# Middle stage of a hybrid encoder: 32x32 triangular blocks on GpSimd, half solves and unnormalised keys and queries

## Chip, cores, metric

One core of one Trainium2 chip. The metric is device time in microseconds of one execution of the whole kernel. The kernel before was run three times: 3174.05, 3177.18 and 3189.18 us, median 3177.18.

## What is computed

One layer over 2,064 prompt rows (16 meta tokens and 2,048 inputs) and 32 sample rows: an input projection with a short causal convolution, a gated delta rule (8 heads of 64) beside a sliding-window attention (8 query heads, 2 key/value heads), an output projection, a layer norm, and a squared-ReLU feed-forward block with a second layer norm. The part that the change touches is the delta rule:

```python
q = l2_normalize(q) * DN_DK ** -0.5 ; k = l2_normalize(k)
A = where(strict, beta[..., :, None] * kk * decay, 0)        # kk = k k^T, decay from the cumulated gates
T = A + eye(chunk)
W = triangular_solve(T, beta * exp(G) * k) ; U = triangular_solve(T, beta * v)
qk = (q k^T) * decay ; q_dec = q * exp(G) ; k_dec = k * exp(G_last - G)
# per chunk:  u = U - W S ;  o = q_dec S + qk u ;  S = exp(G_last) S + k_dec^T u
o = o * rsqrt(mean(o^2) + eps) * norm_w * silu(z)
```

The kernel works in chunks of 128 tokens (a tile), so T is 128x128 for each of 8 heads, and the state goes from tile to tile.

## The kernel before

Three stages run one after the other. The first (project_stage) makes the projections, normalises the input and writes everything to scratch in device memory. The middle one (mix_stage) goes over 18 tiles of 128 tokens, two per round of a hardware loop, the first four and the last two tiles written out. The last (mlp_stage) is the feed-forward block. In the middle stage each engine has its own order of work, written out by hand in a function `step(t)`, and semaphores tie them together; nothing is planned by a program. In step t three tiles are in flight: the delta rule and attention of tile t, the preparation (norms, decays, products of keys) of tile n = t+1, and output projection and layer norm of tile p = t-1 (pp = t-2 for its transposed rows). PSUM has eight banks: inv0, inv1, fr0, fr1, prod, pair, one1, one2.

**The inverse of T.** Its 16x16 diagonal blocks (64 lanes: 8 heads by 8 blocks) are inverted on GpSimd by forward substitution, L1710 to L1723: two operations over 64x256, then 28 small ones, each of which waits for the one before it. The lanes get their blocks through device memory. SyncE, which issues all DMAs in its own order, waits for at_done, writes `at` out (L848), waits for that to land, and reads the diagonal back (L850); after GpSimd's last step it writes the blocks (L858), waits, and reads whole 128x128 rows into `nn` (L862). TensorE and VectorE then build 32x32 and 64x64 inverses in two levels: transpose (L1038), product (L1052), mask (VectorE L1365), product (L1060), update (VectorE L1372); and the last level with 64x64 products (L1074, L1083) and copies (L1378, L1384). `solve` (L1111) multiplies the 128x128 inverse with the right-hand side of each head.

**Keys and queries** are normalised before use: ScalarE squares them, TensorE sums squares over a head with a 128x128 mask matrix (L972), ScalarE takes Ln and Exp (L1553 to L1561), VectorE multiplies (L1295). `spread_gates` (L980) spreads cumulated gates over 128 partitions from 8 rows. `turn_keys` (L1007) transposes keys and values.

**Order on SyncE in a step:** load z, load res of p, store rows of pp, to_lanes(n), store columns of pp, load_front (gates and q/k/v of t+2), from_lanes(n), load_attention of t+2. **Order on GpSimd:** small inverses of n, then `low` twice (L1733, remainder of the mixed rows after rounding, needed by the output projection), then the shift of the layer norm of p (L1740). **Order on TensorE:** the step starts with the transpose of the gates of n (L960), then the inverse's levels are laid between pieces of the output projection of p (three_products, L122 to L124) so that VectorE's and ScalarE's work is covered.

Of the kernel before, what the change touches and what calls it, by code (L numbers as in the profile page):

```python
# [48 lines left out]
LEVELS = (16, 32)  # L49
SMALL = 16  # L50
LANES = HEADS * P // SMALL
LANE_STRIDE = SMALL * P + SMALL
# [618 lines left out]
def mix_stage(nc, io):  # L671

    with ExitStack() as ctx:
        m = Memory(nc, ctx, "b")

        masks = m.sb("masks", [P, 4 + len(LEVELS), P])
        ident, upper, same_head, future = (masks[:, i, :] for i in range(4))
        level_mask = [masks[:, 4 + i, :] for i in range(len(LEVELS))]
        pick = m.sb("pick", [HEADS, HEADS, P])
# [6 lines left out]
        consts = m.sb("consts", [P, 3])  # L686
        lane_masks = m.sb("lane_masks", [LANES, 2, SMALL * SMALL])

        qkv = m.sb("qkv", [P, 12, P])
# [5 lines left out]
        gate = m.sb("gate", [P, 2 * HEADS])  # L695
        cum = m.sb("cum", [P, 2, HEADS])
        cum_row = m.sb("cum_row", [HEADS, P])
# [4 lines left out]
        hat = m.sb("hat", [P, 2, 8, P])  # L702
        at = m.sb("at", [P, 2, HEADS, P])
        work = m.sb("work", [P, HEADS, P])
        nn = m.sb("nn", [P, 2, HEADS, P])
# [3 lines left out]
        lane_a = m.sb("lane_a", [LANES, SMALL, SMALL])  # L709
        lane_n = m.sb("lane_n", [LANES, SMALL, SMALL])  # L710
        lane_t = m.sb("lane_t", [LANES, HD])
# [8 lines left out]
        decay, squares = probs_t[:, 0, :, :], probs_t[:, 1, :, :]  # L720
# [3 lines left out]
        mm = turned_rows[:, :, :, :].rearrange("p a h c -> p (a h c)").rearrange("p (h c) -> p h c", c=P)  # L724
# [18 lines left out]

        def turned_heads(bank, g):

            return fr[bank][:, :].rearrange("p (j g c) -> p g j c", g=2, c=HD)[:, g, :, :]

        def odd_blocks(x, l):

            return x.rearrange("p h (n two b) -> p (h n) two b", two=2, b=LEVELS[l])[:, :, 1, :]  # L750

        def whole(scratch):

            return scratch.rearrange("(h b) x -> h (b x)", h=HEADS)[:, 0:P * P].rearrange("h (p i) -> p h i", i=P)

        def diagonal(scratch):

            return scratch[:, 0:SMALL * P].rearrange("l (j i) -> l j i", i=P)[:, :, 0:SMALL]

        names = """const_in wo_in0 wo_in1 bias_out bias_in zero_out qkv_in att_in z_in res_in h1_out h1t_out state_in state_out  # L760
        at_out lanes_in nn_out nn_in rel_full rel_copied wo_hi_done wo_lo_done zeroed window_added hidden_in hidden_done
        gate_full ss_full cum_full gb_full kk_full qk_full scored kv_turned m_full r_full x_full r_end x_end
        ks_full y_full snew_full oin_full vwin_turned pt_full ont_full pv_full wo_full ost_full h1t_full
        gates_copied cum_copied hat_done em_done at_done qk_scaled lane_steps lanes_done kd_done s_biased soft_steps
        r_masked n_done r_end_done n_final rn_first rn_done qs_scaled u_done s_scaled state_done o_done o_summed
        on_done mixd_done attn_scaled soft_end resid_done ln_halves ln_stats ln_shift ln_gain beta_done
        squared ss_logged rnorm_done gate_exps decay_done m_done v_copied probs_done sink_exp pt_copied
# [6 lines left out]
        L = len(LEVELS)  # L774
        TURNS = 2 * L + 2
# [11 lines left out]
        def _(sp):  # L787
            for dst, src in ((masks[:, :, :], io["masks"]), (pick[:, :, :], io["pick"]), (key_mask[:, :], io["window"]),
                             (gain[:, :], io["ln1_g"].partition_broadcast(P)),
                             (shift[:, :], io["ln1_b"].partition_broadcast(P)), (norm_w[:, :], io["norm_w"]),  # L790
                             (sinks[:, :], io["sinks"].partition_broadcast(P)),
                             (lane_masks[:, :, :], io["lane_masks"]),
                             (probs[0:N_BUCKETS, 0, 0:HEADS], io["table"]),
                             (probs_t[0:N_BUCKETS, 0, 0:3, :].rearrange("p a b -> p (a b)")[:, 0:REL], io["one_hot"])):
                sp.dma_start(dst, src).then_inc(s["const_in"], 16)

            def load_front(t):
                if t.reaches(1):
                    q = t.plus(-1)
                    sp.wait_ge(s["kv_turned"], by(q, 2))  # L800
                    pass_waits(sp, s["passed"])
                    sp.wait_ge(s["hat_done"], by(q, 2))
                here = t.span(P)
                sp.dma_start(gate_rows[:, :], io["gates"][:, here]).then_inc(s["qkv_in"], 16)
                sp.dma_start(qkv[:, :, :], io["proj"][0:12, :, here].rearrange("u p c -> p u c")).then_inc(s["qkv_in"], 16)
# [40 lines left out]
            def to_lanes(t):  # L846
                sp.wait_ge(s["at_done"], by(t, 2))
                sp.dma_start(whole(io["at_lanes"]), at[:, t.parity, :, :]).then_inc(s["at_out"], 16)  # L848
                sp.wait_ge(s["at_out"], by(t, 16))
                sp.dma_start(lane_a[:, :, :], diagonal(io["at_lanes"])).then_inc(s["lanes_in"], 16)  # L850

            def from_lanes(t):
                sp.wait_ge(s["lanes_done"], by(t, 1))
                if t.reaches(1):
                    sp.wait_ge(s["nn_in"], by(t.plus(-1), 16))
                else:
                    sp.wait_ge(s["zero_out"], 48)
                sp.dma_start(diagonal(io["nn_lanes"]), lane_n[:, :, :]).then_inc(s["nn_out"], 16)  # L858
                sp.wait_ge(s["nn_out"], by(t, 16))
                if t.reaches(2):  # L860
                    sp.wait_ge(s["y_full"], by(t.plus(-2), 1))
                sp.dma_start(nn[:, t.parity, :, :], whole(io["nn_lanes"])).then_inc(s["nn_in"], 16)  # L862
# [21 lines left out]
            def step(t):  # L884
# [5 lines left out]
                if t.reaches(1):  # L890
                    load_res(t.plus(-1))
                if t.reaches(2):
# [5 lines left out]
                if m2:  # L898
                    load_front(m2)
                if n:  # L900
                    from_lanes(n)
# [6 lines left out]
                if m2:  # L908
                    load_attention(m2)

# [5 lines left out]
            sp.wait_ge(s["zeroed"], 4)  # L916
            empty = work[0:LANES, :, :].rearrange("p a b -> p (a b)")
            for c in range(0, LANE_STRIDE, D_MODEL):
                width = min(D_MODEL, LANE_STRIDE - c)
                sp.dma_start(io["nn_lanes"][:, c:c + width], empty[:, 0:width]).then_inc(s["zero_out"], 16)  # L920
# [28 lines left out]
        def _(pe):  # L949
# [4 lines left out]
            def turn_gates(t):  # L954
                pe.wait_ge(s["qkv_in"], by(t, 32))
                pass_waits(pe, s["passed"])
                if t.reaches(1):
                    pe.wait_ge(s["vwin_copied"], by(t.plus(-1), 1))
                pass_waits(pe, s["passed"])
                pe.transpose(one2[:, 0:2 * HEADS], gate_rows[:, :], ident[0:2 * HEADS, 0:2 * HEADS]).then_inc(s["gate_full"], 1)  # L960

            def sum_gates(t):
                pe.wait_ge(s["gates_copied"], by(t, 1))
                pe.matmul(one2[:, 0:HEADS], upper, gate[:, 0:HEADS], start=True, stop=True)
                pe.matmul(one2[0:HEADS, P:2 * P], gate[:, 0:HEADS], upper, start=True, stop=True).then_inc(s["cum_full"], 1)

            def norms(t):
                if t.reaches(1):
                    pe.wait_ge(s["s_biased"], by(t, 2, 1) if t is START else by(t.plus(-1), 2, 1))
                for g in range(2):  # L970
                    pe.wait_ge(s["squared"], by(t, 2, g + 1))
                    pe.matmul(fr[g][:, :], same_head, squares[:, 4 * g:4 * g + 4, :].rearrange("p a b -> p (a b)"),  # L972
                              start=True, stop=True).then_inc(s["ss_full"], 1)

            def spread_gates(t):
                pe.wait_ge(s["cum_copied"], by(t, 3))
                for g in range(2):
                    pe.wait_ge(s["ss_logged"], by(t, 2, g + 1))
                    for h in range(4):
                        last = pe.matmul(fr[g][:, h * P:h * P + P], pick[:, 4 * g + h, :], cum_row[:, :], start=True, stop=True)  # L980
                    last.then_inc(s["gb_full"], 1)

            def key_products(t):
                pe.wait_ge(s["hat_done"], by(t, 2))
                pe.wait_ge(s["em_done"], by(t, 6))
                for j in range(4):
                    for g in range(2):
                        k = hat[64 * g:64 * g + 64, t.parity, 4 + j, :]
# [4 lines left out]
            def query_products(t):  # L993
                pe.wait_ge(s["at_done"], by(t, 2))
                for j in range(4):
                    for g in range(2):
                        half = slice(64 * g, 64 * g + 64)
                        last = pe.matmul(fr[g][:, j * P:j * P + P], hat[half, t.parity, 4 + j, :], hat[half, t.parity, j, :],
                                         start=True, stop=True)
                last.then_inc(s["qk_full"], 1)  # L1000

            def turn_keys(t):
                pe.wait_ge(s["qk_scaled"], by(t, 1))
                for g in range(2):
                    for j in range(4):
                        src = hat[:, t.parity, 4 + j, :] if g == 0 else qkv[:, 8 + j, :]
                        last = pe.transpose(fr[g][:, j * P:j * P + P], src, ident)  # L1007
                    last.then_inc(s["kv_turned"], 1)

            def scores(t, first=False):  # L1010
# [3 lines left out]
                else:  # L1014
                    pe.wait_ge(s["kd_done"], by(t, 2))
                    pe.wait_ge(s["v_copied"], by(t, 2))
# [9 lines left out]
            def turn_values(t):  # L1026
                if t.reaches(1):
                    pe.wait_ge(s["o_done"], by(t.plus(-1), 1))
                else:
                    pe.wait_ge(s["cum_copied"], by(t, 3))  # L1030
# [4 lines left out]
            def turn_inverse(t, g):  # L1035

                for h in range(4):
                    last = pe.transpose(inv[g][:, h * P:h * P + P], nn[:, t.parity, 4 * g + h, :], ident)  # L1038
                last.then_inc(s["m_full"], 1)

            def first_inverse(t):
# [1156 lines left out]
```

## Time and profile before

| what | value |
|---|---|
| median of the runs | 3177.18 us (3174.05 to 3189.18) |
| the profiled execution | 3180.55 us; its span 3178.8 us |
| TensorE busy | 2939.2 us (92%) |
| VectorE, ScalarE, GpSimd busy | 1355.9, 1006.3, 1205.9 us |
| granted TensorE clock, mean | 0.963 of full speed |
| middle stage | about 612 to 1654 us from the span's start |

Times in the rows are counted from the start of the span. PE is TensorE, DVE VectorE, ACT ScalarE, POOL GpSimd, SPq the queue of SyncE. A matmul of 32-bit numbers has two records per matmul; the output projection works on halves rounded to fp32r and has one. Busy time is the union of the records, which overlap at their ends.

### The profile page before, as it was taken

To read this page: it belongs to the slowest core of one execution; us is meant where nothing else is said; L and a number is where in the kernel's file an instruction comes from. 1 tells how busy PE (TensorE), PEld (TensorE's weight loads), DVE (VectorE), ACT (ScalarE), POOL (GpSimd) and SP (SyncE) were. 2 spreads that over 40 slices of the span, in tenths; PEclk is the share of its full clock that TensorE was granted. 3 is DMA by queue.
4 is the path that set the end of the run, shared out by engine and by line. 5 is a ranking of instruction groups with operands and counts; after the bars stand their busy time and mean duration, and the time that the engine had idled before them with its cause. 6 is when DMAs were issued, how large, how long until landed. Compare 5 with 4: busy or idle time off the path is not lost. (4 is left out here: it accounts for less than half of the span.)

```text
span 3178.8 us, 50801 instructions
## 1 busy us (share of the span) xinstructions
PE 2939.2 (92%) x18048; PEld 2774.9 (87%) x18048; DVE 1355.9 (43%) x2341; ACT 1006.3 (32%) x2072; POOL 1205.9 (38%) x1282
## 2 busy tenths in 40 slices
PE   5899999729999999999959999999999999999997
PEld 4899999618787878878848999999999999999996
DVE  7643200135656565656625511651363156116502
ACT  4322211324434443444422222222222222222222
POOL 4210101012222222222205555555555555555554
PEclk9899999859999999999978999999999999999998
DMA  5322212252232222233214434444444434444432
GB/s 192 116 86 71 86 67 83 64 136 62 87 88 81 83 84 79 87 93 87 76 50 141 135 124 126 130 143 127 134 134 128 134 110 141 139 130 130 133 113 88
DMA packets 238591, 341.83 MB, mean 108 GB/s; under 512 B 56578, under 2 KB 176322, under 8 KB 235674
## 3 DMA queue, kind: packets, MB, share of 16 engines
q1 hardware_dynamic: 237450, 339.01, 34.5%
q10 hardware_dynamic: 1056, 1.70, 0.2%
q8 instruction: 52, 0.85, 0.1%
q14 instruction: 33, 0.27, 0.0%
HBM read 264.45 MB, written 76.21 MB: 107 GB/s over the span
## 5 line engine op out<-in xcount | busy, mean ns | idle before, releaser
L1949 POOL TENSOR_TENSOR c_w_lo<-c_raw,c_w_hi 128x512 fp32r<-128x512 f32 x640 | 852.3, 1332 | 639.2 <-ACT c_w_hi L1969 639.0
L1969 ACT ACTIVATE c_w_hi<-c_raw 128x512 fp32r<-128x512 f32 x640 | 404.3, 632 | 1057.6 <-PE c_bank L124 1024.9
L122 PE MATMUL c_bank<-c_h_hi,c_w_hi 128*128 128x416 f32 x1280 | 454.1, 355 | 20.7 <-POOL c_w_lo L1949 19.5
L124 PE MATMUL c_bank<-c_h_hi,c_w_lo 128*128 128x416 f32 x1280 | 452.8, 354 | 0.0
L124 PE MATMUL c_bank<-c_mid_hi,c_w_lo 128*128 128x416 f32 x1280 | 450.8, 352 | 0.0
L122 PE MATMUL c_bank<-c_mid_hi,c_w_hi 128*128 128x416 f32 x1280 | 450.2, 352 | 0.0
L123 PE MATMUL c_bank<-c_h_lo,c_w_hi 128*128 128x416 f32 x1280 | 449.1, 351 | 0.0
L123 PE MATMUL c_bank<-c_mid_lo,c_w_hi 128*128 128x416 f32 x1280 | 447.0, 349 | 0.0
L122 PE MATMUL a_bank<-a_h_hi,a_w_hi 128*128 128x420 f32 (+4 forms) x984 | 341.3, 347 | 5.9 <-PEq L168 4.5
L124 PE MATMUL a_bank<-a_h_hi,a_w_lo 128*128 128x420 f32 (+4 forms) x984 | 340.0, 346 | 0.0
L123 PE MATMUL a_bank<-a_h_lo,a_w_hi 128*128 128x420 f32 (+4 forms) x984 | 339.8, 345 | 0.0
L2074 DVE COPY c_out<-c_bank 128x416 f32 x40 | 23.7, 591 | 627.2 <-PE c_bank L124 627.2
L122 PEld LDWEIGHTS c_bank<-c_h_hi,c_w_hi 128*128 128x128 f32 x1280 | 241.9, 189 | 22.6 <-POOL c_w_lo L1949 21.1
L124 PEld LDWEIGHTS c_bank<-c_h_hi,c_w_lo 128*128 128x128 f32 x1280 | 241.7, 189 | 3.3
L123 PEld LDWEIGHTS c_bank<-c_h_lo,c_w_hi 128*128 128x128 f32 x1280 | 241.6, 189 | 2.8
L124 PEld LDWEIGHTS c_bank<-c_mid_hi,c_w_lo 128*128 128x128 f32 x1280 | 240.2, 188 | 3.2
L123 PEld LDWEIGHTS c_bank<-c_mid_lo,c_w_hi 128*128 128x128 f32 x1280 | 240.0, 188 | 2.7
L122 PEld LDWEIGHTS c_bank<-c_mid_hi,c_w_hi 128*128 128x128 f32 x1280 | 240.5, 188 | 0.1
L2021 DVE TENSOR_SCALAR c_positive<-c_bank 128x416 f32<-128x416 f32 x160 | 94.4, 590 | 244.9 <-PE c_bank L124 244.9
L527 POOL TENSOR_TENSOR a_w_lo<-a_raw,a_w_hi 128x1024 fp32r<-128x1024 f32 x20 | 48.3, 2413 | 394.4 <-ACT a_w_hi L543 394.4
L122 PEld LDWEIGHTS a_bank<-a_h_hi,a_w_hi 128*128 128x128 f32 x984 | 188.7, 192 | 9.2 <-issue 5.6
L123 PEld LDWEIGHTS a_bank<-a_h_lo,a_w_hi 128*128 128x128 f32 x984 | 188.6, 192 | 3.1
(221 smaller groups left out, 4479.6 us busy)
## 6 DMA issues: line engine op xcount, KB each, us to landing
c_raw<-in_w_ff SPq DMA_DIRECT2D x320, 512.0 KB, 3.6
scratch_proj<-a_row SPq DMA_DIRECT2D x22, 1152.0 KB, 5.1
b_qkv<-scratch_proj SPq DMA_DIRECT2D x18, 768.0 KB, 5.5
a_raw<-in_w_in SPq DMA_DIRECT2D x23, 512.0 KB
a_x<-in_x SPq DMA_DIRECT2D x18, 512.0 KB, 3.6
scratch_h_rows<-a_h SPq DMA_DIRECT2D x18, 512.0 KB, 2.7
scratch_at_lanes<-b_at SPq DMA_DIRECT2D x18, 512.0 KB, 3.2
b_nn<-scratch_nn_lanes SPq DMA_DIRECT2D x18, 512.0 KB, 4.0
```

The lines of the kernel that those rows point to most:

```text
L122: pe.matmul(out, w_hi, x_hi, start=first, stop=False)
L123: pe.matmul(out, w_hi, x_lo, start=False, stop=False)
L124: return pe.matmul(out, w_lo, x_hi, start=False, stop=last)
L527: pool.tensor_tensor(w_lo[:, p, :, :], raw[:, p, :, :], w_hi[:, p, :, :].bitcast(F32), ALU.subtract).then_inc(w_lo_done, 1)
L1949: pool.tensor_tensor(w_lo[:, p % 2, ks, :], raw[:, p, ks, :], w_hi[:, p % 2, ks, :].bitcast(F32), ALU.subtract).then_inc(w_lo_done, 1)
L1969: act.activation(w_hi[:, p % 2, ks, :], raw[:, p, ks, :], ACT.Copy).then_inc(w_hi_done, 1)
L2021: dve.tensor_scalar(positive[:, :], src, 0.0, None, ALU.max).then_inc(positive_done, 1)
L2074: dve.tensor_copy(out[:, one(c2 * 2 + c), :], bank2[c][:, 0:BLOCK].unsqueeze(1)).then_inc(out_done, 1)
```

## The change

- GpSimd inverts 32x32 blocks: 32 of them (8 heads by 4), each spread over four partitions (SHARES) with eight of its columns each, so 128 partitions. 62 small operations in place of 2 + 28, and one copy (set_lanes) ahead of them.
- The blocks travel in four DMAs each way and leg: `at` out by 32-row blocks, four reads of the same blocks into the four shares, four writes of columns, four reads into `nn`, which now holds 64 columns for each half.
- TensorE pairs 32x32 blocks to 64x64 ones (pair_rows, pair_update, 16 matmuls of 32x32x32 each), VectorE transposes the even blocks (turn_even) and copies (copy_pair_rows, place_pair). The solve goes by halves: solve_head (rows 0 to 63), carry_over (the block of `at` below), take_over on VectorE, solve_rest. The levels of masks are gone.
- Keys and queries stay unnormalised in the products; their lengths enter through the strengths, the values (scale_values) and the factor of the output's norm (o_weighed, o_factor). TensorE transposes q, k and v (q is new), ScalarE squares the transposed rows, VectorE sums (sum_keys, sum_queries). The mask product (L972) and the multiplication (L1295) are gone. qkv has two buffers.
- spread_gates takes its rows from partitions 0 to 7 and 64 to 71 in turn.
- `low` moves from GpSimd to VectorE.
- The orders of all engines are rewritten. SyncE: load_front of t+2 comes ahead of to_lanes(n), and from_lanes(n) comes last, after load_attention. scores now comes ahead of attend.

The core of the diff:

```diff
-LEVELS = (16, 32)
-SMALL = 16
-LANES = HEADS * P // SMALL
+SMALL, SHARES = 32, 4
+LANES = HEADS * BLOCKS32
+LANE_COLS = SMALL // SHARES
...
             def to_lanes(t):
                 sp.wait_ge(s["at_done"], by(t, 2))
-                sp.dma_start(whole(io["at_lanes"]), at[:, t.parity, :, :]).then_inc(s["at_out"], 16)
-                sp.wait_ge(s["at_out"], by(t, 16))
-                sp.dma_start(lane_a[:, :, :], diagonal(io["at_lanes"])).then_inc(s["lanes_in"], 16)
+                for b in range(BLOCKS32):
+                    here = slice(b * SMALL, b * SMALL + SMALL)
+                    sp.dma_start(io["at_lanes"][b * HEADS:b * HEADS + HEADS, :, :].rearrange("h j i -> j h i"),
+                                 at[here, t.parity, :, here]).then_inc(s["at_out"], 16)
+                sp.wait_ge(s["at_out"], by(t, 16 * BLOCKS32))
+                for q in range(SHARES):
+                    sp.dma_start(lane_a[q * LANES:q * LANES + LANES, :, :], io["at_lanes"]).then_inc(s["lanes_in"], 16)
...
             def from_lanes(t):
                 sp.wait_ge(s["lanes_done"], by(t, 1))
+                columns = io["nn_lanes"].rearrange("(c q) l r -> q l c r", q=SHARES)
+                for q in range(SHARES):
+                    sp.dma_start(columns[q], lane_n[q * LANES:q * LANES + LANES, :, :]).then_inc(s["nn_out"], 16)
+                sp.wait_ge(s["nn_out"], by(t, LANE_LOADS))
...
+                for b in range(BLOCKS32):
+                    half = slice(b % 2 * SMALL, b % 2 * SMALL + SMALL)
+                    sp.dma_start(nn[b * SMALL:b * SMALL + SMALL, t.parity, :, half],
+                                 io["nn_lanes"][:, b * HEADS:b * HEADS + HEADS, :]).then_inc(s["nn_in"], 16)
...
+                for j in range(SMALL - 1):
+                    w, n = SMALL - 1 - j, j // SHARES + 1
+                    shape = [P, n, w]
+                    here = lane_n[:, 0:n, j + 1:SMALL]
...
+            def turn_even(t):
+                dve.wait_ge(s["nn_in"], by(t, LANE_LOADS))
+                dve.transpose(nn_even[:, :, :], nn[:, t.parity, :, 0:SMALL]).then_inc(s["even_turned"], 1)
+            def take_over(t):
+                dve.wait_ge(s["low_full"], by(t, 1))
+                dve.tensor_tensor(rn[64:P, :, :], rn[64:P, :, :], heads4(one2, HD)[64:P, :, :], ALU.add).then_inc(s["low_done"], 1)
```

The new order of a step on SyncE, TensorE and VectorE (`if` lines left out):

```python
# SyncE
load_z(t); load_res(p); load_front(t+2); store_rows(pp); to_lanes(n); store_cols(pp); load_attention(t+2); from_lanes(n)
# TensorE
turn_gates(n); turn_rows k, v (n); sum_gates(n); from_state(t); spread_gates(n); turn_queries(n)
output_product(p, 0, ATTENTION); key_products(n); turn_h1(pp, 0); output_product(p, 0, DELTA); pair_rows(t)
turn_h1(pp, 1); output_product(p, 1, ATTENTION); pair_update(t); query_products(n); solve_head(t)
output_product(p, 1, 0:2); carry_over(t); output_product(p, 1, 2:4); solve_rest(t); turn_probs(t, 0 and 1)
state_update(t); output_update(t); scores(n); attend(t); turn_values(n); turn_o(t); turn_attention(t)
# VectorE
copy_gates(n); low(p); copy_sums(n); low(p); sum_keys(n); residue(t); strengths(n); exponents(n); scale_values(n)
sum_queries(n); decayed_keys(n); turn_even(t); residual(p, 0); copy_pair_rows(t); left_keys(n); maxima(t)
place_pair(t); decayed_queries(n); take_over(t); residual(p, 1); update(t); softmax_sums(t); norm_stats(p)
new_state(t); new_output(t); norm_shift(p); sum_squares(t); biased(n); normalise_o(t); norm_gain(p)
scale_attention(t); gate_o(t)
# GpSimd
set_lanes(n); small_inverses(n); h1_rows(p)
```

## Rows read from the trace of the kernel before

**Rows 1.** Engines by stretch: the middle stage's start and its steady part (busy us, records).
```profile
612.00:706.30 94.30, 19.12 (x89) 12.43 (x87) 24.42 (x49) 19.78 (x40) 10.36 (x30) 0.55 0.55 128
805.00:1560.50 755.50, 717.27 (x5781) 611.61 (x5780) 463.87 (x1017) 331.24 (x875) 199.49 (x485) 0.98 0.29 85
```
**Rows 2.** The same view (PE, PEld, DVE, ACT, POOL, PEclk, DMA, GB/s), two steps.
```profile
1010.96:1063.25 52.29, 49.74 (x397) 41.96 (x396) 31.55 (x70) 22.47 (x59) 13.47 (x33) 0.97 0.28 83
1063.25:1113.83 50.58, 48.03 (x396) 41.35 (x395) 31.53 (x70) 22.36 (x59) 13.44 (x33) 1.00 0.30 86
```
**Rows 3.** One line's instructions: the transpose of the gates, one in each step.
```profile
L960 PE MATMUL b_one<-b_masks,b_gate_rows x18: 230/231/256, 636.9 to 1526.4; 16*128 16x16 f32 x18
```
**Rows 4.** Groups of TensorE in 1010.96:1113.83, two steps: count, busy, mean ns, idle before.
```profile
L1052 PE MATMUL b_inv<-b_turned_rows,b_at 128*128 128x128 f32 x64 | 8.2, 281 | 0.0
L1060 PE MATMUL b_inv<-b_nn,b_work 128*128 128x128 f32 x64 | 8.0, 278 | 0.0
...
L1038 PE MATMUL b_inv<-b_masks,b_nn 128*128 128x128 f32 x48 | 6.4, 276 | 2.7 <-DVE b_probs L1341 2.7
L972 PE MATMUL b_fr<-b_probs_t,b_masks 128*128 128x512 f32 x8 | 5.6, 838 | 1.2 <-ACT b_probs_t L1547 1.2
L980 PE MATMUL b_fr<-b_cum_row,b_pick 8*128 8x128 f32 x32 | 4.1, 276 | 0.0
L1102 PE MATMUL b_one<-b_state,b_hat 64*128 64x64 f32 x64 | 4.0, 275 | 0.0
...
L1111 PE MATMUL b_one<-b_rn,b_nn 128*128 128x64 f32 x32 | 3.8, 272 | 0.0
...
L1074 PE MATMUL b_inv<-b_turned_rows,b_at 64*64 64x64 f32 x32 | 2.3, 220 | 0.7 <-ACT b_turned_rows L1584 0.7
```
**Rows 5.** GpSimd in order of time (start, us), smallest and largest steps of one inversion.
```profile
885.59 0.20 POOL L1720 TENSOR_TENSOR b_lane_t<-b_lane_a,b_lane_n 64x14 f32<-64x14 f32 x1
885.87 0.21 POOL L1723 TENSOR_TENSOR b_lane_n<-b_lane_n,b_lane_t 64x14 f32<-64x14 f32 x1
...
889.90 0.29 POOL L1723 TENSOR_TENSOR b_lane_n<-b_lane_n,b_lane_t 64x56 f32<-64x56 f32 x1
890.27 0.28 POOL L1720 TENSOR_TENSOR b_lane_t<-b_lane_a,b_lane_n 64x56 f32<-64x56 f32 x1
```
**Rows 6.** TensorE in order of time: its first record of tile 0's delta rule.
```profile
706.27 1.94 PE L1038 MATMUL b_inv<-b_masks,b_nn 128*128 128x128 f32 x8 [16.50 <-DMA b_nn<-scratch_nn_lanes]
```
**Rows 7.** VectorE and GpSimd in order of time, first tile's inversion.
```profile
694.44 1.24 DVE L1474 TENSOR_TENSOR b_wo_lo<-b_x,b_wo_hi 128x1024 fp32r<-128x1024 f32 x1 [5.98 <-ACT b_wo_hi L1650]
...
694.67 1.14 POOL L1723 TENSOR_TENSOR b_lane_n<-b_lane_n,b_lane_t 64x44 f32<-64x44 f32 x1
```
**Rows 8.** Groups of VectorE in 833:1600 that read two operands from SBUF.
```profile
L1357 DVE TENSOR_TENSOR b_soft<-b_soft,b_sinks 128x8 f32<-128x8 f32 x15 | 20.0, 1336 | 0.5
...
L1470 DVE TENSOR_TENSOR b_x<-b_x,b_gain 128x1024 f32<-128x1024 f32 x15 | 18.2, 1215 | 0.0
```
**Rows 9.** SyncE's queue in order of time: issues around one inversion.
```profile
1031.40 0.38 SPq L848 DMA_DIRECT2D scratch_at_lanes<-b_at  x1
1034.62 0.61 SPq L850 DMA_DIRECT2D b_lane_a<-scratch_at_lanes  x1
...
1040.50 0.43 SPq L804 DMA_DIRECT2D b_gate_rows<-scratch_gates  x1
1041.04 0.99 SPq L805 DMA_DIRECT2D b_qkv<-scratch_proj  x1
```
**Rows 10.** DMA issues in 984:1035: count, KB each, median us from issue to landing.
```profile
b_qkv<-scratch_proj SPq DMA_DIRECT2D x1, 768.0 KB, 5.7
...
b_nn<-scratch_nn_lanes SPq DMA_DIRECT2D x1, 512.0 KB, 4.0
...
scratch_nn_lanes<-b_lane_n SPq DMA_DIRECT2D x1, 64.0 KB, 2.5
```
**Rows 11.** What SyncE's queue waited for in 984:1035 (us, times, longest).
```profile
SPq L848 <- DVE b_at L1312: 13.5, 1, 13.5
```

More of the change, by code:

```diff
@@ L674, in mix_stage @@
         m = Memory(nc, ctx, "b")
[L676 to L679, printed above, removed]
+        masks = m.sb("masks", [P, 3, P])
+        ident, upper, future = (masks[:, i, :] for i in range(3))
+        pick = m.sb("pick", [P, 4, P])
         bias = m.sb("bias", [P, HEADS, SPAN])
@@ L959, in turn_gates, with turn_rows, turn_queries @@
+            def turn_rows(t, bank, first, done):
+                for j in range(4):
+                    last = pe.transpose(bank[:, j * P:j * P + P], qkv[:, t.parity, first + j, :], ident)
+                last.then_inc(done, 1)
+            def turn_queries(t):
+                if t.reaches(2):
+                    pe.wait_ge(s["attn_mixed"], by(t.plus(-2), 1))
                 pass_waits(pe, s["passed"])
-                pe.transpose(one2[:, 0:2 * HEADS], gate_rows[:, :], ident[0:2 * HEADS, 0:2 * HEADS]).then_inc(s["gate_full"], 1)
+                turn_rows(t, pair, 0, s["q_turned"])
@@ L962, in sum_gates @@
             def sum_gates(t):
[L963 to L973, printed above, removed]
+                pe.wait_ge(s["gates_copied"], by(t, 2))
@@ L975, in spread_gates @@
+                pe.matmul(fr[0][:, 0:HEADS], upper, gate[:, 0, 0:HEADS], start=True, stop=True)
+                both = gate[:, :, :].rearrange("p a c -> p (a c)")[:, 0:64 + HEADS]
+                pe.matmul(fr[0][0:64 + HEADS, P:2 * P], both, upper, start=True, stop=True).then_inc(s["cum_full"], 1)
             def spread_gates(t):
                 pe.wait_ge(s["cum_copied"], by(t, 3))
[L977 to L981, printed above, removed]
@@ L1033, in turn_values @@
                 last.then_inc(s["vwin_turned"], 1)
[L1035 to L1041, printed above, removed]
-                pe.wait_ge(s["s_biased"], by(t, 2))
-                pe.wait_ge(s["nn_in"], by(t, 16))
-                pass_waits(pe, s["passed"])
-                for g in range(2):
-                    turn_inverse(t, g)
@@ new lines, in pair_update @@
+            def pair_update(t):
+                pe.wait_ge(s["r_copied"], by(t, 1))
+                pass_waits(pe, s["passed"])
+                for h in range(HEADS):
+                    for e in (0, 64):
+                        even, odd = slice(e, e + SMALL), slice(e + SMALL, e + 2 * SMALL)
+                        last = pe.matmul(inv[0][even, h * SMALL:h * SMALL + SMALL], work[odd, h, :],
+                                         nn[odd, t.parity, h, SMALL:HD], start=True, stop=True)
+                last.then_inc(s["x_full"], 1)
@@ L1154, in attend @@
                     pe.wait_ge(s["attn_mixed"], by(t.plus(-1), 1))
+                if not t.last():
+                    pe.wait_ge(s["squared"], by(t.plus(1), 2))
                 for h in range(HEADS):
```

530 lines of the change are left out of this document (263 added, 267 removed).

## Prediction, made before the changed kernel was run

> **What bounds the kernel now.** I read the engines by stretch first. From 805 to 1560.5 us TensorE is busy for 717.3 of 755.5 us, VectorE for 463.9, ScalarE for 331.2, GpSimd for 199.5 [rows 1]: the steady part of the middle stage is TensorE's. In two single steps it is busy for 49.7 of 52.3 and 48.0 of 50.6 us [rows 2], on average 48.9. The transpose of the gates stands once in each step; from step 1 (754.8 us) to step 16 (1526.4) [rows 3] there are 15 steps of **51.44 us**, so 2.5 us of a step are idle. The wait view of SyncE then shows what slack the blocks' way through memory has: 13.5 us of waiting ahead of their first DMA [rows 11]. So today the lanes are covered, and only TensorE's work counts. The projections ahead and the feed-forward stage behind are not edited; I cost them at nothing.
>
> **TensorE's step after the change.** Gone per step, half of each group's two-step time [rows 4]: level products 4.1 (L1052) and 4.0 (L1060), three transposes of the inverse 3.2 (L1038), sums of squares 2.8 (L972), the full solve 1.9 (L1111), and the 64x64 level, 1.15 (L1074) and as much again for L1083, which has the same shape: 18.3. L980 takes its rows from one part of the array; L1102 alternates between two and does 16 matmuls in 2.0 us, so 8 of them in 1.0: another 1.05 saved. Total 19.35. Added: four transposes of queries, 4/24 of L1038's 3.2, 0.5; the transposes of keys and values only move. Three half solves, each 8 matmuls of 64 columns as in L1074, 3.5. pair_rows and pair_update are 16 matmuls each; no row has 32x32 tiles. The nearest is L1102 with 16 alternating matmuls in 2.0 (upper end, taken); the lower is 0.6, if four tiles overlap where two do there. Together 4.0. So 48.9 - 19.35 + 8.0 = 37.6 busy, and with 2.5 idle as now **40.1 us** a step. The idle is of a new kind: at the end of the step VectorE has biased, normalise_o, norm_gain and scale_attention to do (2048, 512, 1024 and 512 elements at L1470's 1.2 ns, 4.9 us [rows 8]) against attend's 3.8 (twice L1111), and turn_attention waits for the last; norms(n) no longer waits for ScalarE (1.2 and 2.7 us idle per two steps [rows 4]). scores ahead of attend gives `biased` cover and I take nothing for it.
>
> VectorE is at 31.5 us a step [rows 2]. By elements per partition at L1470's 1.2 ns [rows 8], masks, updates, copies and the normalisation that go are 5,120 (6.1 us); `low`, two sums, scale_values, turn_even, pair copies and take_over that come are 4,352 (5.2 us): it stays near 31 and is no bound. ScalarE, 22.4, loses six copies and four passes for the norms. Both are at zero cost, covered by TensorE's 40 us.
>
> **The lanes' loop.** This is the part that I think decides. In the new order SyncE does to_lanes(n), then the rest, then from_lanes(n), and only behind that the next step's z, res, load_front, store_rows, and then to_lanes of the next tile. GpSimd's whole inversion lies between. Nothing of it overlaps with itself, so a step can't be shorter than the way around:
> - a. four writes of `at`. Issues are 0.54 us apart (1040.50 to 1041.04 [rows 9]), so the last starts at 1.6. Small DMAs land in 2.5 us [rows 10]: 4.1 with a free queue. But z, res, gates, q/k/v and rows, 2.06 MB, were issued in the 3.2 us before. q/k/v's 768 KB land in 5.7 us; over the 2.5 of a 64 KB one that is 220 KB a us [rows 10], so they need 9.3 us and the blocks could land at up to 8.6. I take 6.0, between 3.9 and 8.6. Before, both legs took 1034.62 - 1031.40 = 3.2 and some 3 us [rows 9].
> - b. four reads into the shares, 128 KB each: 1.6 + 2.6 = 4.2 (3.7 to 5.6; 5.6 by the 4.0 us of the 512 KB read of nn [rows 10]).
> - c. GpSimd. A step with 14 elements begins 0.28 us after the last, one with 56 after 0.37 [rows 5]: 0.25 + 0.00214 per element. The 31 rounds have 1,560 elements in products and as many in sums: 62 x 0.25 + 3,120 x 0.00214 = 22.2 us, against 11.0 now (28 steps with 1,120 elements, two with 256, by the same formula). Then VectorE gets in the way: at 694.44 it starts a 1.24 us operation on two SBUF operands, and GpSimd's step at 694.67 lasts 1.14 where its like take under 0.3 us [rows 7]; the other way round, L1357 with 8 elements lasts 1336 ns where GpSimd has a long operation [rows 8]. GpSimd will now be busy through the end of the step, where norm_gain (1.22 [rows 8]), two `low` (0.6 each at that rate) and normalise_o (0.6) lie. That is 3.0, and small ones; I add 3.3: 25.5 (22.2 to 29).
> - d. four writes of columns 1.6 + 2.4 = 4.0 (3.7 to 5.2). e. four issues into nn, 2.1.
> - f. z, res, gates, q/k/v, rows: four at 0.54 and one of 0.99 [rows 9], 3.2. They count, since they stand ahead of the next to_lanes. load_attention waits for scores and turned values at the end of the step; by then GpSimd is still at work, so it costs nothing.
>
> Sum 6.0 + 4.2 + 25.5 + 4.0 + 2.1 + 3.2 = **45.0 us**, ends 38.8 and 53.7. That is above 40.1: the stall will be at turn_even, which waits for nn_in, with pair_rows behind it on TensorE (residual(p, 0) and the rest of VectorE's step too). TensorE's halved clock after such a stall lies in the slack of 4.9 us.
>
> The Trainium skill, "SBUF — State Buffer", section "Who interferes with whom", says that GpSimd shares a port pair with VectorE and that the holder locks it for its whole instruction. Rows 7 and 8 agree. Without such a lock the loop would be 3.3 us shorter, 41.7.
>
> **From step to time.** nn of tile 0 arrives at 706.3 now [rows 6]. New: 11.2 us more of GpSimd and 3.7 more for the four legs (4.1 + 4.2 + 4.0 + 4.1 with a free queue, against 3.2 + 3 + 2.5 + 4.0): 721; nothing else of step 0 is later. From there 17 rounds lead to tile 17's. Now the stage ends (1654) 73 us after 706.3 + 17 x 51.44 = 1581. Of these, 12 lie ahead of turn_even in the new order (gates, transposes, from_state, spread_gates, queries, key products, two pieces of the output projection), and some 5 of the inverse's work is gone: 56. So it ends at 777 + 17 T. With T = 45.0: 1542, **112 us less**. The sum is made against the profiled execution, 3180.55 us, 3.4 above the median of the runs: 3180.6 - 112 - 3.4 = **3065**.
>
> **Rivals.**
> 1. *TensorE is still the bound* (0.22). The legs are at their low ends and VectorE hardly disturbs GpSimd; the loop is below 42.3. Against: the burst of 2 MB just ahead of to_lanes, and the order on SyncE. T from 40.1 to 42.3 gives 877 - 17 T = 195 to 158 less: 2982 to 3019.
> 2. *Slower* (0.05). Place: the same loop, GpSimd's 62 dependent steps. They now run on 128 partitions and beside VectorE; if one costs 0.50 instead of 0.36 us, c is 34 and T 54 us. That decides from T = 52.5 on, by 877 - 17 x 52.5 = -16 us; at 54 it is 41 longer: 3218. For: such a step has 0.25 us of fixed cost that I know from 64 partitions only. Against: L1474 cost one GpSimd step per operation, not all of them.
> 3. *No difference* (0.04): T between 50.7 and 52.5; legs at 8.6, 5.6 and 5.2 us with c at 26 to 28. Time within 3161 to 3193.
> 4. *Fewer gains* (0.11): T from 48.5 to 50.7, 3124 to 3161: the same causes, milder.
> 5. *The pairing doesn't save what it says* (0.03): 32x32 tiles cost several times L1102's time, so that TensorE needs above 45 after all; with 4.5 us each, T = 45.1. The time is then as forecast, but the idle time is gone.
>
> **Chances and range.** The forecast itself, T from 42.3 to 48.5, 3019 to 3124, has 0.55. The range takes it and the better part of rival 1, down to T = 40.5: 2988 to 3125, about 0.8. What my measurement can tell from no change is about 0.5%, 16 us. Faster by more: forecast, rivals 1, 4 and 5, 0.91; within: 0.04; slower: 0.05.
>
> **What would show it.** The transpose of the gates should come every 45 us. GpSimd's inversion should take 24 to 27 us, with some steps stretched to 1.2 us beside VectorE. SyncE's queue should no longer wait for at_done (now 13.5 us); VectorE's longest wait should be turn_even's for nn, 4 to 5 us, and TensorE should be at 37 to 38 us a step with a stall ahead of pair_rows. If the gates come every 40 to 41 us and SyncE waits for at_done, rival 1 is right. If they come at more than 52, the forecast is wrong in c or a. If the first or the last stage moves by over 5 us, something that I cost at nothing counts.

## The result, and the profile after

The changed kernel takes **3078.49 us** (median of 4, 3076.74 to 3079.91) against 3178.26 for the kernel before (4 runs): ratio **0.9681, interval 0.9656 to 0.9706**. Some 100 us are gone, where 112 were forecast. The profiled execution is the one of 3079.91 us, its span 3078.1 us; all rows of the changed kernel are from it.

First the engines by stretch (columns as in [rows 2]): the start of the middle stage until about the time when tile 0's inverses arrive, the rest of step 0, fifteen steps, the last two tiles, and the feed-forward stage.

```profile
612.00:712.60 100.60, 17.93 (x94) 13.63 (x94) 24.11 (x52) 15.87 (x37) 21.95 (x64) 0.50 0.47 108
712.60:762.76 50.16, 32.84 (x307) 29.47 (x307) 28.34 (x64) 15.85 (x48) 17.29 (x61) 0.60 0.26 71
762.76:1429.10 666.34, 588.10 (x5558) 486.28 (x5557) 442.62 (x1052) 270.92 (x808) 326.75 (x941) 0.93 0.33 92
1429.10:1556.00 126.90, 89.78 (x724) 73.08 (x723) 55.30 (x119) 36.35 (x97) 35.27 (x88) 0.82 0.22 64
1556.00:3078.00 1522.00, 1475.17 (x7840) 1458.14 (x7840) 578.63 (x886) 419.07 (x684) 858.32 (x643) 0.98 0.40 128
```

The third and the fourth stretch of the kernel before, in the same view:

```profile
754.80:1526.40 771.60, 733.08 (x5919) 625.44 (x5918) 473.67 (x1037) 335.10 (x883) 201.83 (x494) 0.98 0.29 84
1526.40:1654.00 127.60, 104.47 (x770) 88.84 (x770) 61.28 (x121) 42.78 (x106) 27.48 (x40) 0.90 0.20 63
```

So fifteen steps gave 105.3 us (771.6 to 666.3), the start cost 8.0 (762.8 against 754.8), the last two tiles gave 0.7 and what follows 2.7 (to the ends of the spans, 3178.8 and 3078.1). The step is (1429.1 - 762.76) / 15 = **44.42 us**, by the transpose of the gates as in [rows 3]:

```profile
L960 PE MATMUL b_fr<-b_masks,b_gate_rows x18: 201/229/285, 634.4 to 1429.1; 16*128 16x16 f32 x18
```

TensorE is busy for 588.1 / 15 = 39.2 us of a step, so it stands idle for 5. Where, its waits in the two steps 1027.17:1115.34 say:

```profile
PE b_prod L122 <- DVE b_x L1462: 4.9, 2, 2.8
PE b_pair L1152 <- DVE b_turned_rows L1451: 2.4, 2, 1.2
PE b_inv L1043 <- DVE b_nn_even L1369: 2.1, 2, 1.2
PE b_pair L1182 <- POOL b_h L1758: 0.8, 2, 0.5
```

And the lanes' loop, by SyncE's queue in order of time (start, us):

```profile
1034.44 1.82 SPq L858 DMA_DIRECT2D scratch_nn_lanes<-b_lane_n  x4
1037.48 1.78 SPq L866 DMA_DIRECT2D b_nn<-scratch_nn_lanes  x4
1039.46 0.41 SPq L828 DMA_DIRECT2D b_z<-scratch_proj  x1
1040.14 0.36 SPq L833 DMA_DIRECT2D b_res<-scratch_h_rows  x1
1040.84 0.34 SPq L802 DMA_DIRECT2D b_gate_rows<-scratch_gates  x1
1041.27 0.39 SPq L803 DMA_DIRECT2D b_qkv<-scratch_proj  x1
1041.76 1.20 SPq L837 DMA_DIRECT2D scratch_h_rows<-b_h  x1
1043.10 3.81 SPq L848 DMA_DIRECT2D scratch_at_lanes<-b_at  x4
1049.50 1.71 SPq L852 DMA_DIRECT2D b_lane_a<-scratch_at_lanes  x4
...
1077.83 1.82 SPq L858 DMA_DIRECT2D scratch_nn_lanes<-b_lane_n  x4
```

The distances are the terms of the forecast's sum. Columns to nn, 1034.44 to 1037.48: d, 3.0. To the next load, e: 2.0. Five issues until 1043.10, f: 3.6. The writes of `at` until they have landed, 1049.50, a: 6.4. The reads until GpSimd's first step at 1053.56, b: 4.1. The inversion until 1077.83, c: 24.3. Together 43.4 us, in a step of 43.6. This lap is one of the shorter ones. Over the fifteen laps from 764.05 to 1436.91, read off SyncE's and GpSimd's records in the same way, the means are d 3.1, e 2.2, f 3.8, a 7.0 (4.9 to 8.3), b 4.2 and c 24.4, together 44.9. That this way around is what sets the step, and not a wait for the other engines inside it, the waits of SyncE's queue in 1000:1200 show:

```profile
SPq L129 <- PE b_inv L1023: 60.2, 5, 12.5
SPq L858 <- POOL b_lane_n L1746: 28.0, 4, 7.4
SPq L852 <- DMA scratch_at_lanes<-b_at: 17.1, 5, 3.9
```

The longest of them, 12 us a step for the scores (L1023) ahead of load_attention, lies within GpSimd's inversion: behind it SyncE still waits 7 us a step for GpSimd (L858) with everything else done. In the whole view there is no wait for at_done, where [rows 11] had 13.5 us.

VectorE's and GpSimd's records in order of time show c at work:

```profile
1067.98 1.31 DVE L1478 TENSOR_TENSOR b_x<-b_x,b_gain 128x1024 f32<-128x1024 f32 x1
1068.29 1.17 POOL L1746 TENSOR_TENSOR b_lane_n<-b_lane_n,b_lane_t 128x60 f32<-128x60 f32 x1
1071.93 0.70 DVE L1483 TENSOR_TENSOR b_mix_lo<-b_mixed,b_mix_hi 128x512 fp32r<-128x512 f32 x1 [0.65 <-ACT b_mix_hi L1655]
1072.17 0.61 POOL L1746 TENSOR_TENSOR b_lane_n<-b_lane_n,b_lane_t 128x48 f32<-128x48 f32 x1
```

A sum of 60 elements, some 0.31 us elsewhere, takes 1.17 while VectorE multiplies by the gain, and one of 48 takes 0.61 beside `low`. Both end 0.15 to 0.17 us after VectorE's operation.

### The profile page after: what moved, and what is told of

The parts are those of the page before. It is cut to its first block and busy times, and to the rows that moved or that the text cites. A ratio compares the mean times of both kernels' runs of the same rounds, so it can differ in the third digit from the quotient of the medians.

```text
span 3078.1 us, 50884 instructions
## 1 busy us (share of the span) xinstructions
PE 2768.6 (90%) x17616; PEld 2613.3 (85%) x17616; DVE 1324.5 (43%) x2361; ACT 928.9 (30%) x1982; POOL 1358.6 (44%) x1840
## 5 line engine op out<-in xcount | busy, mean ns | idle before, releaser
L1743 POOL TENSOR_TENSOR b_lane_t<-b_lane_a,b_lane_n 128x60 f32<-128x60 f32 (+24 forms) x558 | 175.2, 314 | 385.4 <-DMA b_lane_a<-scratch_at_lanes 343.1
L527 POOL TENSOR_TENSOR a_w_lo<-a_raw,a_w_hi 128x1024 fp32r<-128x1024 f32 x20 | 48.3, 2414 | 394.4 <-ACT a_w_hi L543 394.4
```

The lines of the kernel that those rows point to most:

```text
L527: pool.tensor_tensor(w_lo[:, p, :, :], raw[:, p, :, :], w_hi[:, p, :, :].bitcast(F32), ALU.subtract).then_inc(w_lo_done, 1)
L1743: pool.tensor_tensor(term, lane_a[:, j, j + 1:SMALL].unsqueeze(1).to_broadcast(shape), lane_n[:, 0:n, j].unsqueeze(2).to_broadcast(shape), ...
```

## The experiments

Ratios are to the kernel before, run on the same chip as the version in question. "Step" is the distance of the gates' transposes over fifteen steps of the profiled execution. The first four versions ran on one chip, the next four (from the short loop to `low` back on GpSimd) on another, and the last three (the two with the state's load moved, and `low` on top) on a third.

**Is it the loop?** Two edits of SyncE's order and two of size. First, undo one move:

```diff
-                if m2:
-                    load_front(m2)
                 if t.reaches(2):
                     store_rows(t.plus(-2))
                 if n:
                     to_lanes(n)
                 if t.reaches(2):
                     store_cols(t.plus(-2))
+                if m2:
+                    load_front(m2)
```

> One part of the change undone: SyncE issues the loads of gates and q/k/v of t+2 behind to_lanes and the store of the columns, as before the change. Theory L (the lanes' loop through SyncE and GpSimd sets the step, 44.4 us): the loop loses the issue of two DMAs (1 us) and 776 KB of backlog ahead of the blocks (about 2 us); a step of 41 to 42 us, 3020 to 3045 us in all against 3078. Rival R (TensorE's own chain sets the step, lengthened by VectorE's wait for the rows of the residual, 3.3 us a step): these rows are issued where they were, so 3065 to 3080.

Measured: 3030.1 us, ratio 0.9512 (0.9476 to 0.9547), step 41.02. The loads of gates and q/k/v, put back where they stood before, are worth 3.4 us a step. SyncE's queue:

```profile
1061.55 0.41 SPq L828 DMA_DIRECT2D b_z<-scratch_proj  x1
1062.26 0.36 SPq L833 DMA_DIRECT2D b_res<-scratch_h_rows  x1
1062.81 0.37 SPq L837 DMA_DIRECT2D scratch_h_rows<-b_h  x1
1063.81 2.69 SPq L848 DMA_DIRECT2D scratch_at_lanes<-b_at  x4
1069.12 1.71 SPq L852 DMA_DIRECT2D b_lane_a<-scratch_at_lanes  x4
```

Here f is 2.3 and a 5.3. Over fifteen laps f fell from 3.8 to 3.3, its wait for at_done included, and a from 7.0 to 4.2: the burst cost twice, by its issues and, for the greater part, by holding up the four writes behind it. SyncE now waits a little for at_done too (5.0 us in 5 times in 1000:1200), so the loop and the other engines are about even.

Next, take the loop away: 16 of the 31 rounds of the inversion (the later columns stay unfinished).

> GpSimd does 16 of the 31 rounds of the inversion; the last 15 rounds (30 operations) are left out, so the blocks are inverted only in part. Theory L: the loop loses 30 x 0.25 + 1400 x 0.00214 = 10.5 us and is no longer the bound; the step falls to TensorE's own 39.5 to 41.5 us, 3000 to 3030 us in all, and SyncE waits for at_done again. Rival R: GpSimd's time is covered, 3065 to 3080.

Measured: 2961.9 us, ratio 0.9298 (0.9263 to 0.9333), step 38.51, below the 3000 to 3030 us and 39.5 to 41.5 us that were expected. SyncE waits for at_done again (12.1 us in 5 times in 1000:1200). So 38.51 is what the other engines need with GpSimd out of the way, 1.6 us less than the 40.1 of the forecast.

Then lengthen TensorE's work instead: output_update done twice over (its second pass writes the same values), 1.85 us.

> TensorE does output_update twice (the same 8 matmuls again into the same bank, 1.85 us more in each of 18 steps). Theory L: TensorE has some 4.5 us of slack against the loop, so the time stays within 8 us of the changed kernel's. Rival R: TensorE's chain is the bound, 1.85 x 17 = 31 us more, 3105 to 3112.

Measured: 3092.5 us, ratio 0.9712 (0.9672 to 0.9751), step 45.10. Of 1.85 us, 0.68 show. If TensorE were the bound, all would. The intervals of the two ratios overlap, so that anything shows at all rests on the step alone. Still, the whole kernel is 10 us slower by the ratios and 14 by the medians, not within the 8 that theory L gave, and SyncE now waits for at_done (15.0 us in 5 times in 1000:1200, up to 5.0): in some steps the slack is used up.

**Which order serves the loop?** All loads of the next step are put ahead of from_lanes, into the time in which SyncE waits for GpSimd:

> SyncE issues z, res and the gates and q/k/v of t+3 ahead of from_lanes, while it would wait for GpSimd, in place of between from_lanes and the next to_lanes. Theory L: the loop loses four issues (2.9 of its 3.7 us) and most of the backlog (1.5 to 2 us) and falls to 39 to 40; TensorE's own 40 to 41.5 us bind; 3010 to 3035 us. The rows of the residual are there early too, so their wait of 3.3 us goes. Rival R: also faster, by 3.3 x 17 = 56 us at most, 3022 or more; SyncE would still not wait for at_done.

Measured: 3015.0 us, ratio 0.9469 (0.9432 to 0.9506), step 40.20. The loads then stand in front of the writes of columns, and d grows from 3.0 to about 5:

```profile
1090.10 0.39 SPq L803 DMA_DIRECT2D b_qkv<-scratch_proj  x1
1090.92 2.02 SPq L858 DMA_DIRECT2D scratch_nn_lanes<-b_lane_n  x4
1095.85 1.78 SPq L866 DMA_DIRECT2D b_nn<-scratch_nn_lanes  x4
```

So only the small ones go there, and q/k/v goes where it was before, behind the loop's first half:

```diff
-                load_z(t)
-                if t.reaches(1):
-                    load_res(t.plus(-1))
-                if m2:
-                    load_front(m2)
                 ... store_rows, to_lanes, store_cols
+                if m2:
+                    load_front(m2)
                 ... load_attention
+                    load_z(n)
+                    load_res(t)
                     from_lanes(n)
```

> As e1 (gates and q/k/v of t+2 behind to_lanes), and z and res of the next step go out ahead of from_lanes. Theory L: between from_lanes and the next to_lanes only store_rows is left; the loop is 1.4 us shorter than e1's 41.3 and the residual's rows are in time, while GpSimd's way out isn't held up by a large load as in e4. A step of 39 to 40 us (e1 41.0, e4 40.2), so 25 us less than e1's 3030, 3000 to 3012 us. If the two halves of the loop share what is won (the blocks wait for at_done by now), at least 10 us less than e1.

Measured: 3015.5 us, ratio 0.9467 (0.9439 to 0.9495), step 40.40: the same as the version above, and a little above the 3000 to 3012 us expected. SyncE now waits for at_done (1000:1200):

```profile
SPq L848 <- DVE b_at L1316: 13.8, 5, 3.8
```

The loop has 2.8 us of slack a step, and the step is still 1.9 above 38.51. TensorE's waits in this version:

```profile
PE b_pair L1152 <- DVE b_turned_rows L1451: 5.9, 5, 1.2
PE b_fr L995 <- DVE b_ends L1301: 5.0, 4, 1.8
```

Both are VectorE being late, with its end of the step and with the start of the next. So scale_attention, for which turn_attention (L1152) waits, is put ahead of norm_gain (1.2 us), which nobody on TensorE waits for so early:

```diff
                 normalise_o(t)
+                scale_attention(t)
                 if chain:
                     norm_gain(p)
-                scale_attention(t)
                 gate_o(t)
```

> As e5, and VectorE does scale_attention ahead of norm_gain. Theory: with the loop short, TensorE's wait of 1.2 us for the scaled attention at the end of each step counts: 10 to 20 us less than e5. Rival: the shift of the layer norm (h1_rows, on GpSimd, then the transposes of its rows) comes later by 0.7 us and takes it back: within 5 us of e5.

Measured: **2991.7 us, ratio 0.9399 (0.9372 to 0.9425)**, step 38.75. Both waits are gone. Two swapped lines give 24 us here. They also make the loop the bound again, at a shorter lap. In 1000:1200 SyncE waits for at_done once, and for GpSimd in every lap:

```profile
SPq L858 <- POOL b_lane_n L1746: 23.5, 6, 4.1
SPq L848 <- DVE b_at L1316: 0.6, 1, 0.6
```

The laps there are 38.0 us long (d 3.0, e 2.2, f 0.6, a 3.4, b 4.2, c 24.6), and TensorE is busy for 73.5 of 75.9 us (1035.93:1111.86): the two are about even.

**How much is the two engines' contention for SBUF?** In the changed kernel norm_gain is done on one column in place of 1,024 (the gain is left out of the result elsewhere):

> The changed kernel with norm_gain over one column in place of 1024 (the gain of the first layer norm is left out elsewhere). It isn't on the lanes' loop. If VectorE's operations on two SBUF operands stop GpSimd's steps for their whole length (theory), GpSimd's inversion gets 1.1 to 1.3 us shorter and the step with it: 15 to 22 us less than the changed kernel. Without such a lock: within 5 us, since the loop doesn't wait for VectorE.

Measured: 3065.1 us, ratio 0.9624 (0.9599 to 0.9650), step 43.45, 0.97 less. GpSimd's inversion, first to last step, is 24.36 us in the changed kernel (mean of seven, 24.12 to 24.66) and 23.52 here (23.31 to 23.99): 0.84 of the 0.97.

**Why did the last two tiles gain nothing?** The longest of TensorE's waits in 1429:1560 of the changed kernel, and what SyncE waits for at from_lanes of the last tile (1460:1560), then the same line in the kernel before (1530:1660):

```profile
PE b_one L1069 <- DMA b_state<-in_state_delta: 12.2, 1, 12.2
SPq L858 <- POOL b_lane_n L1746: 24.1, 1, 24.1
```
```profile
SPq L858 <- POOL b_lane_n L1723: 8.3, 1, 8.3
```

TensorE's wait is new. The sample's state is loaded at the start of the last step, and from_lanes of the last tile stands ahead of it on SyncE in both kernels. What grew is the wait in from_lanes, with GpSimd's longer inversion. Here the load goes ahead of it:

```diff
-                if t.last():
-                    change_state()
...
+                    if n.last():
+                        change_state()
                     from_lanes(n)
```

> The last two tiles' stretch, from the gates of tile 17 at 1429.1 to the end of the middle stage at 1556, is 127 us in the changed kernel, as in the one before (127.6), where 17 us less were forecast. In it from_state (L1069) waits 12.2 us for the DMA that loads the sample's state. SyncE issues that load only behind from_lanes of the last tile, which now stands last in the step. Here this one pair of DMAs (state out, state in) is issued ahead of from_lanes of the last tile; nothing else is changed. Theory Q (queue order): the 12.2 us wait goes, TensorE then does from_state, spread_gates and one piece of the output projection earlier and waits at turn_even for nn, whose issue at 1482 does not move; 6 to 11 us less than the changed kernel, ratio to before near 0.965 to 0.966. Rival: nn, which is issued at 1480.66 to 1482.4, is as late as the state at 1484.3, and the stall only moves whole to L1043: under 3 us less, ratio 0.968.

Measured: 3069.9 us, ratio 0.9648 (0.9628 to 0.9669); the wait is gone, and the state goes out at 1465.86 us instead of 1482.49. The spans are 3068.1 against 3078.1 with about the same step (44.55). The intervals overlap; the wait that vanished is the evidence. On the fastest version:

> The same move of the state's load on top of the fastest version so far (front's load back behind the stores, z and res ahead of from_lanes, scale_attention ahead of norm_gain; ratio 0.9399), whose wait of L1069 for the state is 15.2 us. Theory Q: 8 to 13 us less, ratio near 0.936 to 0.9375, time 2979 to 2984. Rival as above: the stall moves to L1043, under 3 us less.

Measured: 2986.1 us, ratio 0.9386 (0.9366 to 0.9405), not to be told from 0.9399. There TensorE comes earlier, the state is still late, and 8.5 us of the 15.2 remain. The load now stands behind load_z of the next tile, where SyncE waits 19.7 us for VectorE's last operation on `mixed` (L1440, in 1370:1470); whether that is what remains was not tried.

**What did moving `low` bring?** It goes back to GpSimd, behind the inversion:

```diff
 # GpSimd
                     small_inverses(n)
+                low(t, ATTENTION, 1)
+                low(t, DELTA, 2)
                 if t.reaches(1):
```

> One part of the change undone: the remainders of the mixed rows are made on GpSimd again, behind the inversion of n. Theory L: they aren't ahead of from_lanes, so the loop itself is the same or 1.2 us shorter, but mix_lo comes 3 us later than TensorE wants it, and with it key_products, at_done and to_lanes: the step gets 1 to 3 us longer, 10 to 45 us more than the changed kernel. Rival: its time is hidden by the slack, within 10 us of the changed kernel or faster.

Measured: 3073.5 us, ratio 0.9653 (0.9627 to 0.9679), step 43.44; the inversion 23.53 us (mean of seven). The ratio's interval overlaps with that of the changed kernel; the 10 to 45 us more that theory L expected are not there. The theory that gave `low` on VectorE a value was wrong here: GpSimd waits some 15 us a step for its lanes and has room for the 2.7 us, and its inversion is no longer stretched by VectorE's `low`.

The same edit on the fastest version, the one with the state's load moved:

> The version above with low back on GpSimd behind the inversion. In the changed kernel that took 0.98 us off a step by shortening GpSimd's inversion from 24.4 to 23.5 us, since VectorE's low stretched two of its steps. Theory L (that time counts only through the lanes' loop): the loop is no longer the bound here, so the step stays at 38.5 to 38.9 us and the time within 5 us of the version above. Rival: VectorE's end of the step, which low lengthens by 1.3 us, is what TensorE waits for: 0.3 to 1 us per step less, 5 to 15 us less in all.

Measured: 3020.7 us, ratio 0.9491 (0.9471 to 0.9510), against 2986.1 without it: **34.5 us slower**, step 40.86 against (1346.6 - 761.66) / 15 = 39.0. Neither theory had that, and both took the loop to be no longer the bound, which the trace of the version without this edit contradicts: in 1000:1200 SyncE never waits for at_done there, and 23.3 us in 6 times for GpSimd. GpSimd and TensorE in order of time:

```profile
1055.22 2.68 POOL L1745 TENSOR_TENSOR b_mix_lo<-b_mixed,b_mix_hi 128x512 fp32r<-128x512 f32 x2
```
```profile
1056.63 0.49 PE L122 MATMUL b_prod<-b_wo_hi,b_mix_hi 128*128 128x512 f32 x1 [1.17 <-POOL b_mix_lo L1745]
...
1057.52 0.63 PE L122 MATMUL b_prod<-b_wo_hi,b_mix_hi 128*128 128x512 f32 x1
1057.95 0.63 PE L123 MATMUL b_prod<-b_wo_lo,b_mix_hi 128*128 128x512 f32 x1
```

With TensorE early, `low` is late by 1.2 us, and behind this stall the matmuls come 0.43 us apart in place of 0.23 for seven of them, with a little more at both ends: 1.6 us more. The granted clock over 800:1300 is 0.93, and 0.98 without the edit. With it at_done is late: SyncE waits for it 19.4 us in 5 times in 1000:1200, so the 0.8 us that GpSimd's inversion is shorter (23.8 against 24.6) don't count. So the change's placing of `low` on VectorE is worth nothing in the changed kernel and some 34 us once the loop is short.

## Why the prediction was right, and where it was not

**What decides: right.** The forecast said that the way SyncE, GpSimd, SyncE sets the step. Half the rounds take 5.9 us off it, 1.85 us more of TensorE add 0.7, and the loop's parts add up to the step. Rival 1 (TensorE the bound) said that SyncE would wait for at_done; in 1000:1200 it doesn't at all. The slower rival, 0.50 us for a GpSimd step, is out: a step of 60 elements takes 0.31 us on 128 partitions, where [rows 5] have 0.28 to 0.29 for 56 elements on 64.

**The sum, term by term** (forecast, mean of fifteen laps): a 6.0, 7.0; b 4.2, 4.2; c 25.5, 24.4; d 4.0, 3.1; e 2.1, 2.2; f 3.2, 3.8; together 45.0, 44.9, and by the gates 44.4. The sum is this close by luck: c and d were taken 1.1 and 0.9 too high, a and f 1.0 and 0.6 too low. a: the burst ahead of the writes holds them up longer than the 6.0 that I chose between 3.9 and 8.6. c: 3.3 us for VectorE's interference was too much; inversions take 24.36, the free value was 22.2, so 2.2. I charged norm_gain and the two `low` at 1.2 us each, their own duration; by the two experiments they cost 0.84 and 0.83. The blocked sum does its own 0.3 us of work as well: 1.17 less 0.31 is 0.86. d: writes of 32 KB in four DMAs land in 1.6 us, not 2.4.

The Trainium skill, "SBUF — State Buffer", section "Who interferes with whom", has the port pair locked for the holder's whole instruction. The trace agrees: the stretched sums end 0.15 to 0.17 us after VectorE's operation does, and 0.84 us of the inversion went with norm_gain.

**TensorE's step: the total right, by two errors.** Busy time was forecast at 37.6 us; with scale_attention moved it is 561.1 / 15 = 37.4. (In the changed kernel itself it is 39.2, outside the 37 to 38 named as a sign: the three lines of the output product, 43.3 us in two steps against 38.8 in the kernel before, run in part at the lower clock behind the stalls.) But pair_rows and pair_update, taken at the upper end of 2.0 us each, measure 0.7, by TensorE's groups in two steps of the version with scale_attention moved:

```profile
L1053 PE MATMUL b_inv<-b_nn,b_work 32*32 32x32 f32 x64 | 1.4, 192 | 0.0
L1043 PE MATMUL b_inv<-b_nn_even,b_at 32*32 32x32 f32 x64 | 1.4, 191 | 1.5 <-DVE b_nn_even L1369 1.5
```

So the lower end, 0.6, was nearly right, but not for its reason, four tiles that overlap: each of the two functions, like L1102, alternates between two parts of the array. Records of 0.19 us come 0.02 us apart; why, no run here shows. What balanced most of it: I subtracted the busy times of groups. In two steps of each kernel all of TensorE's groups add up to 62.1 us a step before and 48.3 with scale_attention moved, 13.8 less, while the busy time falls from 48.9 to 36.8, 12.1 less, since a group's rows overlap its neighbours' at the ends. Subtracting groups takes too much off. The idle time of 2.5 us was too high also: the engines' own bound is 38.5, not 40.1.

**"TensorE's halved clock after such a stall lies in the slack": only while there is slack.** In the changed kernel it does. In the version with a short loop and `low` on GpSimd, a stall of 1.2 us cost 1.6 more by the clock, and the step grew by 1.9. The forecast's "VectorE at zero cost" holds in the same way only there: once the loop had 2.8 us of slack, TensorE still stood 1.9 above its bound through two waits for VectorE.

**A wait that I did not see:** VectorE's longest is not turn_even's for nn (6.6 us in 3 times), but residual's for `res`, 17.2 in 5:

```profile
1040.85 0.45 DVE L1369 STREAM_TRANSPOSE b_nn_even<-b_nn 128x256 f32<-128x256 f32 x1 [2.26 <-DMA b_nn<-scratch_nn_lanes]
1043.95 0.69 DVE L1462 SCALAR_TENSOR_TENSOR b_x<-b_res,b_prod 128x512 f32<-128x512 f32 x1 [2.66 <-DMA b_res<-scratch_h_rows]
```

I counted the issue of `res` in f, but not that `res` itself now comes late for its reader. 4 to 5 us was forecast for one wait, and two in a row make 4.9. In the loop-bound kernel this costs nothing of its own: the loop doesn't go through residual.

**From step to time: where the 12 us are.** The fifteen steps gave 105.3 us (forecast 15 x 6.44 = 97). The start cost 8.0, not 15. The inversion of tile 0 is longer as charged, but SyncE begins it sooner:

```profile
668.28 2.59 SPq L848 DMA_DIRECT2D scratch_at_lanes<-b_at  x4
```
```profile
668.82 2.34 SPq L920 DMA_DIRECT2D scratch_nn_lanes<-b_work  x3
...
673.89 0.62 SPq L848 DMA_DIRECT2D scratch_at_lanes<-b_at  x1
```

The second fence is the kernel before: its three writes that clear the lanes' memory are gone with the change, and I hadn't counted that. The last two tiles were to give 30 and gave 0.7. That is the step that failed: "Now the stage ends 73 us after ...: 56". nn of the last tile landed at 1483.8 and the stage ended at 1556, 72 us later. The 56 took the work ahead of turn_even as done before nn comes, but from_state, which stands first in it, waited for the state until 1486.5, and that work ended at 1497.7. TensorE's busy time there fell by 14.7 us, its idle time rose by 14.0 (23.1 to 37.1), 12.2 of that the wait for the state. In the prediction's own terms: the 11.2 us more of GpSimd were charged to the loop and to the start alone, and not to what stands behind from_lanes in SyncE's queue, change_state. That the total came out within 12 us of the forecast is again in part luck: the steps, the start and what follows gave 8, 7 and 3 us more than forecast against the 29 missing here.

In the last two tiles the granted clock is 0.82 against 0.90. Behind the wait for the state from_state takes 3.68 us where it takes 2.00 a step earlier (1430.69), and six output products come up to 0.2 us further apart than at full speed: together some 3 us. What stays open: the remaining wait for the state in the fastest version wasn't tried any further.

## What to carry to other kernels

When a chain through one queue and one slow engine is the bound, write down its parts in order and ask of every instruction in that queue whether it must stand inside the chain: here two loads (776 KB) in the wrong half cost some 50 us, and three reorderings without new work took the ratio from 0.968 to 0.940. Then look again at everything that had been free: `low` on VectorE was worth nothing under the long loop and 34 us under the short one, where two swapped lines, untested under the long loop, gave 24. And check the last steps of a pipeline by themselves: a wait that grows in a queue holds up everything behind it, and there that was a load that other steps don't have.

## What I had not expected of the hardware

- Four issues of DMAs take SyncE 1.8 us with a free queue and 3.81 behind 2 MB of other transfers just issued: the burst holds up the issuing itself, not only the landing.
- Sixteen matmuls of 32x32x32 that alternate between two 32x32 parts of the array take 0.7 us, where L1102's sixteen take 2.0 [rows 4].
- Output products behind two idle stretches of 1.2 and 2.1 us: five come at full speed (0.39 us a record), the next seven at 0.63, and then 0.40 again. In four-microsecond windows of the changed kernel (1040 to 1052; it is 1.00 from there on) the granted clock is:

```profile
1040.00:1044.00 4.00, 1.56 (x38) 1.03 (x36) 0.49 (x2) 0.60 (x1) 0.00 (x0) 1.00 0.83 267
1044.00:1048.00 4.00, 3.21 (x10) 2.64 (x11) 3.92 (x6) 0.00 (x0) 0.00 (x0) 0.75 1.02 293
1048.00:1052.00 4.00, 3.91 (x66) 2.96 (x66) 2.67 (x8) 1.58 (x6) 0.00 (x0) 0.82 0.35 111
```

Here it falls while TensorE is busy again, not in the idle stretch, so a stall's price is larger than its idle time: seven matmuls at 0.2 us more each, 1.4 us on top of 3.2. Behind the 12.2 us wait for the state it has fallen before work resumes (0.50 in 1482:1486, with TensorE idle), and the whole of from_state is slow.
